# A ring of ten weight buffers instead of nine in a two-layer decoder trunk on Trainium2

## The reference, cut to what matters

```python
for i in range(DEPTH):
    mk, mv = memory_kv(mem, mem_norm[i], w_mem_kv[i])
    hn = rms_norm(x, norm_mix[i])
    mixed = rglru_mixer(hn, mk, mv, ...) if i % 2 == 0 else dsa_mixer(hn, mk, mv, ...)
    x = x + mixed @ w_out[i]
    x = x + hier_moe(rms_norm(x, norm_ffn[i]), ...)
# hier_moe, per expert e and its tokens xb:
#   (silu(xb @ w_gate[e]) * (xb @ w_up[e])) @ w_down[e]
```

## Time and profile before

| | us |
|---|---|
| three runs, median | 1558.89 |
| three runs, lowest and highest | 1555.86, 1560.49 |
| the profiled execution, its own time | 1562.51 |
| the profiled execution, span of its core | 1560.6 |
| PE busy in that span | 1428.0 (92%) |
| DVE, ACT, POOL busy | 599.3, 332.1, 103.3 |

### The profile page before, as it was taken

How to read it: one execution, slowest core, us unless ns; L and a number is a source line. 1 busy time by engine, 2 the same in 40 slices (tenths; PEclk the granted TensorE clock), 3 DMA queues, 4 the chain that set the end, 5 groups by cost and what they waited for, 6 DMA issues and landing times.

```text
span 1560.6 us, 16585 instructions
## 1 busy us (share of the span) xinstructions
PE 1428.0 (92%) x6233; PEld 627.5 (40%) x6233; DVE 599.3 (38%) x1094; ACT 332.1 (21%) x620; POOL 103.3 (7%) x199
## 2 busy tenths in 40 slices
PE   5999889599999989999799979995999999899997
PEld 4433545433333333333364545453333333333332
DVE  2563212423343332333349965124333433322333
ACT  3266311011111110111126755110111111110110
POOL 1000100110000000000000123002000000000000
PEclk9999999599999999999999989995999999999998
DMA  8700144499999999999720020544999999999993
GB/s 314 237 0 0 54 193 198 185 379 427 425 426 427 428 427 427 430 426 428 302 92 1 21 92 1 206 171 176 406 426 427 426 428 428 427 428 426 428 428 151
DMA packets 56249, 457.36 MB, mean 293 GB/s; under 512 B 15468, under 2 KB 20124, under 8 KB 31240
## 3 DMA queue, kind: packets, MB, share of 16 engines
q1 hardware_dynamic: 49108, 447.81, 69.4%
q0 software_dynamic: 5504, 8.68, 1.5%
q10 hardware_dynamic: 1588, 0.20, 0.1%
HBM read 459.50 MB, written 10.53 MB: 301 GB/s over the span
## 4 chain that ended last, share of the span: by engine, by line
PE 71%; DMA 21%; DVE 3%; ACT 2%; issue 1%; ACTq 1%; POOL 0%; DVEq 0%; SPq 0%; POOLq 0%
PE ps L1055 22%; PE ps L1359 20%; DMA arena<-in_moe_w_gate 14%; PE ps L1373 10%; PE ps L1381 7%; DMA arena<-in_moe_w_up 6%; PE ps L1305 2%; PE ps L1145 2%; PE ps L1352 2%; PE ps L1064 1%; PE ps L1244 1%; PE ps L1285 1%; PE ps L1365 1%; DMA mix<-scratch_xn,idx 0%; PE ps L1342 0%
## 5 line engine op out<-in xcount | busy, mean ns | idle before, releaser
L1359 PE MATMUL ps<-arena,xT 128*64 128x512 f32 x2048 | 461.7, 604 | 33.3 <-DMA arena<-in_moe_w_gate 27.3
L1359 PEld LDWEIGHTS ps<-arena,xT 128*64 128x64 f32 x2048 | 149.0, 139 | 329.5 <-issue 325.5
L1906 DVE TENSOR_TENSOR x<-ps,x 128x1024 f32<-128x1024 f32 x128 | 156.2, 1224 | 231.7 <-PE ps L1381 229.1
L1373 PE MATMUL ps<-arena,xT 128*64 128x512 f32 x1024 | 226.8, 595 | 0.0
L1381 PE MATMUL ps<-mix,xT 128*128 128x512 bf16 x768 | 179.7, 384 | 5.7 <-ACT mix L1014 5.7
L1055 PE MATMUL ps<-xT,arena 128*128 128x512 f32 x384 | 168.7, 595 | 1.1 <-issue 1.1
L1381 PEld LDWEIGHTS ps<-mix,xT 128*128 128x128 bf16 x768 | 70.6, 99 | 134.7 <-issue 52.6
L1373 PEld LDWEIGHTS ps<-arena,xT 128*64 128x64 f32 x1024 | 70.7, 137 | 131.8 <-issue 127.9
L1055 PE MATMUL ps<-arena,mix 128*128 128x512 f32 x256 | 112.7, 600 | 3.3 <-DMA arena<-in_w_out 2.6
L1055 PEld LDWEIGHTS ps<-xT,arena 128*128 128x128 f32 x384 | 72.0, 190 | 94.2 <-issue 92.6
L1899 DVE TENSOR_TENSOR mix<-ps,mix 128x512 f32<-128x512 f32 x64 | 44.3, 691 | 169.0 <-ACT mix L1011 169.0
(11 more groups left out here) (230 smaller groups left out, 1131.1 us busy)
## 6 DMA issues: line engine op xcount, KB each, us to landing
arena<-in_moe_w_gate SPq DMA_DIRECT2D x64, 2048.0 KB, 29.8
arena<-in_moe_w_up SPq DMA_DIRECT2D x64, 2048.0 KB, 31.1
arena<-in_moe_w_down SPq DMA_DIRECT2D x64, 2048.0 KB, 31.8
arena<-in_lru_w_in SPq DMA_DIRECT2D x2, 3072.0 KB, 16.5
arena<-in_dsa_w_in SPq DMA_DIRECT2D x1, 5120.0 KB, 15.6
arena<-in_w_mem_kv SPq DMA_DIRECT2D x2, 2048.0 KB, 9.0
scratch_xn<-arena SPq DMA_DIRECT2D x8, 512.0 KB, 8.0
arena<-in_w_out SPq DMA_DIRECT2D x1, 4096.0 KB, 13.6
```

The source lines that it names most:

```text
L1359: ins = pe.matmul(ps[e * CAP:(e + 1) * CAP, bank, :], tokT[:, k, e * CAP:(e + 1) * CAP], rows_in[u][:, k, :], start=k == 0, stop=k == KD - 1)
L1373: ins = pe.matmul(ps[e * CAP:(e + 1) * CAP, BANK_Y + c, :], hT[:, j, e * CAP:(e + 1) * CAP], rows_down[u][:, j, c * 512:(c + 1) * 512], st ...
L1906: dve.tensor_tensor(x[:, t, :], ps[:, b:b + 2, :].rearrange("p a n -> p (a n)"), x[:, t, :], ALU.add).then_inc(s_, 1)
```

## The change

The arena grows to ten units. The 16 KB per partition for it come from: the software DMA queue's scratch, cut from 16384 to 4096 bytes; the memory keys and values of layer 0, moved into the arena (words 13600 to 14623), so that `memKT` and `memV` hold one layer only; the transposed parameters `prm`, also moved there; and small constant tiles packed into two (`fixed`, `whole`). The router's logits, which used the keys of layer 0 as their place, get a tile of their own.

The transposed memory `memT[1]` moves from the end of the arena to word 14624, out of the output weights' place. So layer 0's `w_out` is loaded by one DMA early (4 MB at the place of L555) and the late load with its wait (L570, L571) is gone. The normalised rows `xn_ffn` and layer 1's projection weights move from unit 6 on to unit 7 on.

Unit 6 is now free before the expert stage, so seven matrices instead of six are issued at its start; the three after the row stores stay three (j = 1 to 3 of pair 1), and j = 4 and 5 wait for the gate product of pair 0. The slot waits are rewritten for distance ten. PE writes six pairs out and loops over ten, five per iteration; SP writes out pairs 0 and 1 and the last four, and loops over ten.

```diff
--- before.py
+++ after.py
@@ -58,7 +58,7 @@
 NBLK = S // CAP
 OVMAX = 2 * S // CAP
 NP = NE // 2
-NU = 9
+NU = 10
 R = NG + NE
 BIG = -1.0e30
 TAKEN = -3.0e38
@@ -280,31 +280,27 @@
         ones_b = sb("ones_b", [P, P], BF16)
         iota_tok = sb("iota_tok", [P, S])
         iota_e = sb("iota_e", [P, NE])
-        thr = sb("thr", [P, NBLK - 1])
-        rank_w = sb("rank_w", [P, NG])
-        tokid = sb("tokid", [P, NT])
-        place1 = sb("place1", [P, 1])
-        prm = sb("prm", [P, NPRM])
-        eps = sb("eps", [P, 1])
         gains = sb("gains", [P, 6, KD])
         w_route = sb("w_route", [P, KD, R])
         b_route = sb("b_route", [P, 2, R])
-        memKT = sb("memKT", [P, 2, 2, M])
-        memV = sb("memV", [P, 2, 2, XW])
+        memKT1 = sb("memKT", [P, 2, M])
+        memV1 = sb("memV", [P, 2, XW])
+        route_logits = sb("route_logits", [P, NT, R])
         small = sb("small", [P, 256])
 
         soft = small[:, 16:64].rearrange("p (b c h) -> p b c h", b=3, c=4)
         choice = sb("choice", [P, NT, NE], BF16)
-        dest = sb("dest", [P, 2, NT], I32)
         pay = sb("pay", [P, 2, NT, 2])
         tabP = sb("tabP", [P, NP + 1, 2])
         cur = sb("cur", [P, 2])
-        idx = sb("idx", [P, 1], I32)
-        ov_code = sb("ov_code", [P, 2], I32)
         ov_list = sb("ov_list", [1, 2 * OVMAX], I32)
-        ov_n = sb("ov_n", [1, 1], I32)
         ov_cur = sb("ov_cur", [P, 2])
-        ov_idx = sb("ov_idx", [CAP, 1], I32)
+        fixed = sb("fixed", [P, 24])
+        thr, rank_w, tokid = fixed[:, 0:NBLK - 1], fixed[:, 8:8 + NG], fixed[:, 12:12 + NT]
+        place1, eps = fixed[:, 16:17], fixed[:, 17:18]
+        whole = sb("whole", [P, 16], I32)
+        dest = whole[:, 0:2 * NT].rearrange("p (k t) -> p k t", k=2)
+        idx, ov_code, ov_idx, ov_n = whole[:, 8:9], whole[:, 9:11], whole[0:CAP, 11:12], whole[0:1, 12:13]
         ps = ctx.enter_context(nc.psum_tensor("ps", [P, 8, 512], F32))
 
         def area(at, *shape, dt=F32):
@@ -320,12 +316,16 @@
 
         w_out = area(AREA - KD * D, KD, D)
         start_area = area(AREA - KD * D, KD * D)
-        w_in = [area(AREA - KD * D - KD * W0, KD, W0), area(6 * UNIT, KD, W1 - IH)]
+        w_in = [area(AREA - KD * D - KD * W0, KD, W0), area(7 * UNIT, KD, W1 - IH)]
         lo0 = AREA - KD * D - KD * W0
 
         w_kv = [area(0, KD, 2 * XW), area(AREA - KD * D - 6144, KD, 2 * XW)]
         mem = area(4096, 2, D)
-        memT = [area(6144, KD, M), area(AREA - 2 * D, KD, M)]
+        memT = [area(6144, KD, M), area(14624, KD, M)]
+        memKT = [area(13600, 2, M), memKT1]
+        memV = [area(14112, 2, XW), memV1]
+        prm = area(14624 + KD * M, NPRM)
+        assert lo0 >= 14624 + KD * M + NPRM
         bucket_oh = start_area[0:NB, 0:S + P]
         bucket_bias = start_area[0:NB, 640:640 + HEADS]
         bias_rows = start_area[0:HEADS, 1024:1024 + S + P]
@@ -357,7 +357,7 @@
         oT = area(att[1] + 5 * 4 * S, 2, 4 * P)
         relu = mix[:, 0:3, :]
         score = [None] + [mix[:, 2 + q, :] for q in range(1, NT)]
-        xn_ffn = area(6 * UNIT, NT, D)
+        xn_ffn = area(7 * UNIT, NT, D)
 
         rows_in = [area(u * UNIT, KD, FE) for u in range(NU)]
         rows_down = [area(u * UNIT, KF, D) for u in range(NU)]
@@ -508,14 +508,12 @@
             def pair_weights(L, j, u, p, n, first=False):
 
                 if not first:
-                    if j == 0:
+                    if j in (0, 1):
                         sp.wait_ge(m["up_psum"], n + (-1))
-                    elif j in (1, 2):
+                    elif j in (2, 3):
                         sp.wait_ge(m["y_psum"], n * 2 + (-2))
-                    elif j in (3, 4):
+                    else:
                         sp.wait_ge(m["gate_psum"], n)
-                    else:
-                        sp.wait_ge(m["up_psum"], n)
                 weights(L, p * 2 + j % 2, j // 2, u, landed[u])
 
             for L in range(2):
@@ -552,10 +550,9 @@
 
                     sp.wait_ge(tab_zero, 32)
                     sp.wait_ge(bias_stored, 16)
-                    sp.dma_start(w_out[:, 0:6, :], a["w_out"][L].rearrange("(c p) n -> p c n", p=P)[:, 0:6, :]).then_inc(ld["wout"], 16)
                 else:
                     wait_filled(sp, f"1.q.{NC - 1}")
-                    sp.dma_start(w_out, a["w_out"][L].rearrange("(c p) n -> p c n", p=P)).then_inc(ld["wout"], 16)
+                sp.dma_start(w_out, a["w_out"][L].rearrange("(c p) n -> p c n", p=P)).then_inc(ld["wout"], 16)
                 if L:
                     wait_filled(sp, "0.route.3")
                 sp.dma_start(w_route[:, :, 0:NG], a["moe_w_group"][L].rearrange("(p k) n -> p k n", k=KD)).then_inc(ld["wr"], 16)
@@ -567,29 +564,28 @@
 
                     wait_filled(sp, f"0.gate.{NC - 1}")
                     sp.dma_start(w_kv[1], a["w_mem_kv"][1].rearrange("(p k) n -> p k n", k=KD)).then_inc(ld["wkv"], 16)
-                    wait_filled(sp, "1.memV.1")
-                    sp.dma_start(w_out[:, 6:8, :], a["w_out"][L].rearrange("(c p) n -> p c n", p=P)[:, 6:8, :]).then_inc(ld["wout"], 16)
 
                 wait_filled(sp, f"{L}.out.0.0")
                 for j in range(6):
                     pair_weights(L, j, j, 0, NP * L, True)
+                pair_weights(L, 0, 6, 1, NP * L + 1, True)
                 for t in range(NT):
                     sp.wait_ge(rows_normed, rows[L, "ffn", t])
                     sp.dma_start(scratch_xn[L][t * P:(t + 1) * P, :], xn_ffn[:, t, :]).then_inc(xn_stored, 16)
                 wait_filled(sp, f"{L}.out.{NT - 1}.1")
                 sp.wait_ge(xn_stored, 16 * NT * (L + 1))
                 wait_filled(sp, f"{L}.fT.{NT - 1}.1")
-                for j in range(3):
+                for j in range(1, 4):
                     pair_weights(L, j, 6 + j, 1, NP * L + 1, True)
-                for j in range(3, 6):
+                for j in (4, 5):
                     pair_weights(L, j, (6 + j) % NU, 1, NP * L + 1)
                 sp.wait_ge(chosen, 2 * L + 2)
                 sp.dma_start(scratch_ov.ap()[L], ov_code[0:OVMAX, :]).then_inc(ov_stored, 16)
-                with sp.Fori(0, (NP - 4) // 3) as i:
-                    for r in range(2, 5):
+                with sp.Fori(0, (NP - 6) // 5) as i:
+                    for r in range(2, 7):
                         for j in range(6):
-                            pair_weights(L, j, (6 * r + j) % NU, i * 3 + r, i * 3 + (NP * L + r))
-                for p in (NP - 2, NP - 1):
+                            pair_weights(L, j, (6 * r + j) % NU, i * 5 + r, i * 5 + (NP * L + r))
+                for p in range(NP - 4, NP):
                     for j in range(6):
                         pair_weights(L, j, (6 * p + j) % NU, p, NP * L + p)
                 sp.wait_ge(ov_stored, 16 * (L + 1))
@@ -813,13 +809,13 @@
                     row_norm(L, "mem", 2, lambda t: mem[:, t, :], lambda t: xn[:, t, :], mem_ready)
                 row_norm(L, "mix", NT, lambda t: x[:, t, :], lambda t: xn[:, t, :], x_ready)
 
-                kraw = memKT[:, L, :, :].rearrange("p a b -> p (a b)")
+                kraw = memKT[L][:, :, :].rearrange("p a b -> p (a b)")
 
                 def memory_raw(ML, i):
                     if i < 2:
-                        raw(ML, f"memK.{i}", memKT[:, ML, i, :], M)
+                        raw(ML, f"memK.{i}", memKT[ML][:, i, :], M)
                     else:
-                        raw(ML, f"memV.{i - 2}", memV[:, ML, i - 2, :], XW)
+                        raw(ML, f"memV.{i - 2}", memV[ML][:, i - 2, :], XW)
 
                 if L == 0:
                     for i in range(4):
...
@@ -1305,7 +1301,7 @@
                                 ins = pe.matmul(b, v_sb[:, s, :], PT_sb[:, m_ % 2, s, :], start=s == 0, stop=s == qb)
                             ins.then_inc(filled, 1)
 
-                pe.wait_ge(ld["wout"], 32 + 16 * L)
+                pe.wait_ge(ld["wout"], 16 * (L + 1))
                 wait_emptied(pe, f"{L}.xo.{NT - 1}")
                 if L == 0:
                     pe.wait_ge(lru_y, NC)
@@ -1430,11 +1426,11 @@
                 tokens_T(m["xt_psum"])
                 pair(n0, ring(0), landing(0), first=True)
                 pair(n0 + 1, ring(1), landing(1), second=L == 0)
-                pair(n0 + 2, ring(2), landing(2))
-                pair(n0 + 3, ring(3), landing(3))
-                with pe.Fori(0, (NP - 4) // 3) as i:
-                    for r in range(4, 7):
-                        pair(i * 3 + (n0 + r), ring(r), [i * 2 + v for v in landing(r)])
+                for r in range(2, 6):
+                    pair(n0 + r, ring(r), landing(r))
+                with pe.Fori(0, (NP - 6) // 5) as i:
+                    for r in range(6, 11):
+                        pair(i * 5 + (n0 + r), ring(r), [i * 3 + v for v in landing(r)])
                 combine_of(n0 + NP - 1, (0, 1, 2, 3))
 
                 o = ov[L]
...
@@ -1748,7 +1744,7 @@
 
                 rt = route_area
 
```

(5 more changed lines are left out.)

5 lines of the change are left out of this document (2 added, 3 removed).

## The result

Six runs of the changed kernel took 1548.20 to 1553.83 us, median **1551.05 us**; six runs of the kernel before on the same chip took 1555.86 to 1563.30, median 1559.21. The ratio is 0.9943, 95% interval 0.9929 to 0.9957: 8.2 us by the medians, where 13.5 were forecast. The sign and the mechanism came as forecast, and 1551.05 lies within the range, 1 us from its upper end. The profiled execution took 1553.83 us (before: 1562.51), its span is 1552.0.

What follows compares the result with a forecast made beforehand. The expert stages were taken as a race that weight loads decide from pair 8 on, at a full DMA share. Gains of 9.8 + 2.0 + 1.7 = 13.5 us gave a median of 1545.4 us, range 1541 to 1552.

Steps and rivals of the forecast that it cites:

- Change 1: Expert stages: with ten matrices in the ring, 82 instead of 83 remain to load; gain 4.9 us per layer, 9.8 in two.
- rival B: Start of the expert-stage race: a hole in the DMA stream loses the matrix gained; 1555.2 us, chance 0.07.
- Change 2: Layer 0's output projection: w_out in one piece removes PE's wait for the late load; gain 2.0 us, between nothing and 2.6.
- change 3: Start of layer 0's output projection: after a shorter pause PE's clock no longer drops to 0.50; gain 1.7 us, bounds 0 and 1.7.
- Rivals A and D: A: clock drop at the output projection stays, 1547.1 us, chance 0.26. D: nothing is gained there or in races, 1558.9, chance 0.03.
- Change 4: POOL's gathers: the smaller software scratch costs 0, bounds -0.5 and +2 us, since gathers would still land in time.
- Change 5: Expert pairs: PE's longer unrolled code costs 0, up to 1 us for more bytes on the same DMA engines; fetching is hidden.

## Why the prediction was right in kind and its gain too large by 5.3 us

The races, sorted by slots and by pairs of PE code a layer:

```
slots, pairs of code     layer 0                  layer 1                  both, mean
nine, 7                  423.65 423.09 423.41     422.64 423.18 422.31     846.1
nine, 10                 424.42                   421.88                   846.3
ten, 6                   418.88 418.66            417.61 417.83            836.5
ten, 11 (0) and 6 (1)    418.81                   417.64                   836.5
ten, 11                  419.49 419.66 419.71     419.49 419.18 418.94     838.8
ten, 16                  420.23                   418.04                   838.3
```

**Change 1, the tenth buffer: right.** Compared at the nearest lengths of code (seven and six pairs), it shortens the races by 846.1 - 836.5 = 9.6 us; the forecast was 9.8. At long code (ten and eleven pairs) it is 846.3 - 838.8 = 7.5, with one profile of the former; the last part of this section says what lies between. The means of the runs are 1556.5 for the ring of nine with all else of the change and 1547.1 for the eleven runs with ten slots and short code, 9.4 apart; taken each against the kernel before of its own batch, 8.6. The load left out measured the matrix's price by itself, 5.0 and 5.3 us. DMA did not run dry: the loads at 311.50, 318.54 and 328.01 keep the rhythm, and the windows over the races show a full share (rival B is out). The prediction called the DMA engines nearly idle in the stages before, which rows 1 do not say (185 to 379 GB/s from the sixth slice to the ninth); there was room for the seventh matrix all the same. The rule of the Trainium skill that was weighed (DMA: Bandwidth & Descriptors, section Anatomy of one DMA), taken as fixed cost plus bytes for each matrix in turn, would have given 13.6 us; the 9.6 measured speaks against reading it so in a filled queue.

**Change 2, w_out in one piece: right,** and change 3 about right. The wait of 2.62 us became 0.56. By means of runs the late load costs 2.8 us on the changed kernel, and changes 2 and 3 with the small scratch bring 2.9 on nine slots (1559.4 against 1556.5), where 3.7 were forecast. Change 3 took the drop of the clock as certain before; of four profiles with the late load three show it (29.43 us) and one does not (27.73), of ten without it none. By these few profiles its mean is rather three quarters of 1.7 us. Rivals A and D are out.

**Change 4, the scratch: right at nothing,** 0.9996, with a pause of POOL that was not foreseen and hits nobody.

**Change 5, the longer code: this is the term that failed.** It was taken as 0 with up to 1 us. The argument was that the period of the straight pairs equals the loop's, 27.66 us. But those pairs run early, while PE sets the pace and the loads have slack; a cost to the DMA stream doesn't show there, it shows at pair 15. With ten slots the races are 2.3 us shorter with six pairs of code than with eleven (838.65 to 838.98 against 836.49 twice). Most of it comes from layer 1: with the code of that layer alone shortened the sum is already 836.45. By the means of the runs the short code is 4.3 us faster (1551.4 and 1547.1, interval 2.3 to 6.3); taken each against the kernel before of its own batch it is 3.5 us (1.2 to 5.8). The races explain 2.3 of that, and the rest is not placed and may be scatter.

The difference to the forecast is then 0.4 us at the buffer, 0.8 at changes 2 to 4 and 4.3 at the code: of 13.5 us, 8.0 are left (1559.4 to 1551.4). These three come from one chain of means, 1559.4, 1556.5, 1547.1, 1551.4, so that they add up by construction and don't confirm one another.

That the median lies in the range is partly luck: the bounds made room for 1 us of code, not for 4, and the changed kernel's second median, 1552.37, would have been outside.

**How the code costs it** shows in part in the 16 signals of each load. The start of a race scatters, and so does the lag of its last engine; the mean of the 16 signals hardly does. This is the time from that mean at the 41st matrix to that mean at the 92nd, beside the packets of instructions that the trace has in between (the kernel with short code in layer 1 alone stands in the last row but one for layer 0 and in the first for layer 1; the two kernels that leave out a load or the gathered rows are not in it):

```
kernels                                       packets   layer 0, us        layer 1, us
ten slots, 6 pairs of code                    0         255.79 to 255.81   254.77 to 254.79
nine slots, 7 pairs                           1         255.88 to 255.89   254.84 to 254.87
nine slots, 10 pairs                          4         256.18             255.15
ten slots, 11 pairs                           5         256.25 to 256.29   255.21 to 255.29
ten slots, 16 pairs                           9         256.61             255.59
```

Each packet costs 0.09 us, in both layers, with nine slots and with ten. That is a little more than its 1.07 us on one of 16 engines, 0.07. So there is a price per packet. Eleven pairs against six pay 0.45 us of it a race, 0.9 of the 2.3. Against the kernel before, the change has four packets more in each race, 0.7 us in both; that alone would have been inside the bound of 1 us.

The rest of a race's length is where the mean stands at the 41st matrix and how far the last engine is behind the mean at the 92nd. With eleven pairs against six these are on average 0.26 and 0.45 us more a race. With nine slots, ten pairs against seven, the sum of the races seemed to show no cost: the packets cost 0.29 us a race and the last engine's lag 0.41, and an earlier 41st matrix, by 0.60, hid both. Between kernels with equal code that place differs by up to 0.8 us, so this was chance of one profile as far as the record shows.

**What stays open** is the lag of the last engine. In layer 1 it is 3.0 to 3.2 us with eleven pairs in five profiles, 2.2 to 2.4 with six in three, but 2.1 with sixteen; in layer 0 it is 3.2 to 3.7 with eleven, 3.3 to 3.5 with six and 4.3 with sixteen. (The profile without gathers is left out.) It does not follow the length of the code alone; whether it follows which engine the packets meet was not tested. The gap at the start of the span (17.00 against 15.77 us) is scatter: four other kernels with eleven pairs of code in layer 0 took 15.5 to 15.8 there.

## What to carry to other kernels

In a race between loads and computation, count the transfers that remain once the queue is full, and price a buffer at its bytes over the rate of the full queue; that was right to 2% in the races at nearly equal code, and to 4 or 12% by the runs, without or with each batch's own kernel before. A cost that seems hidden where computation sets the pace must be looked for again at the end of the stage that the loads decide. Such a cost is read better from the mean of a load's 16 signals than from the start that waits for the last: it repeated to 0.1 us where the races scatter by up to 0.9. When a ring grows, shorten the unrolled code again: a loop over one period of the ring after the first pair brought 2.3 us in the races and 3.5 to 4.3 in all, on top of the 8 of the change.

## What was not expected of the hardware

- The 16 signals of one matrix drift apart under load, in layer 0 from about 1 us between the first and the last to 7.4 to 7.9 us at the 92nd with six or seven pairs of code, 8.1 to 8.9 with eleven and 9.5 to 9.9 with ten or sixteen, on nine slots and on ten; 3.7 when the gathers move no rows.
- A 16 KB packet of instructions makes the loads of a full queue 0.09 us later on average, in both layers and with both rings.
- Gathered rows cost more than their bytes: 10.7 us a layer where 8.7 would be their share at 427 GB/s.
- Two products of 64 columns each, interleaved into the two halves of the output's partitions, take 0.22 us a record; one after the other 0.43 at the same clock.
- Stalls of 2.0 to 2.6 us before a product were followed by a fall of the clock in three profiles of four at the same place; idle times of 0.56 us there in none of ten.
